# Order of transposes and scores inside an attention step

## The reference

```python
logits = jnp.einsum('bqhd,bkhd->bhqk', q_blk.astype(jnp.float32), kf) * inv_sqrt_d
mask = (key_pos[None, :] < q_pos[:, None])[None, None]
log_beta = jax.nn.log_sigmoid(logits)
log_1m_beta = jnp.where(mask, jax.nn.log_sigmoid(-logits), 0.0)
later = lax.cumsum(log_1m_beta, axis=3, reverse=True) - log_1m_beta
wts = jnp.where(mask, jnp.exp(log_beta + later), 0.0)
return jnp.einsum('bhqk,bkhd->bqhd', wts, vf)
```

## Time and profile before

| | us |
|---|---|
| median of 3 runs | 1737.72 |
| lowest, highest | 1737.65, 1739.27 |
| span of the profiled execution | 1737.0 |
| stage 3 in it, about | 391 to 1367 |
| PE busy in the span | 1674.7 |
| DVE busy in the span | 1156.6 |

### The profile page before, as it was taken

How to read it: one execution, slowest core, us unless ns; L and a number is a source line. 1 busy time by engine, 2 the same in 40 slices (tenths; PEclk the granted TensorE clock), 3 DMA queues, 4 the chain that set the end, 5 groups by cost and what they waited for, 6 DMA issues and landing times. The chain is left out here.

```text
span 1737.0 us, 26738 instructions
## 1 busy us (share of the span) xinstructions
PE 1674.7 (96%) x8430; PEld 1384.2 (80%) x8430; DVE 1156.6 (67%) x1632; ACT 816.9 (47%) x1650; POOL 495.2 (29%) x436
## 2 busy tenths in 40 slices
PE   8999999997999999999989999999999889999998
PEld 6878888886887877888877888878888668888886
DVE  7737400008998899998889988999988674333323
ACT  4412221115676665666656766756766542111111
POOL 3521111104343243242332332432411251505040
PEclk9999999999999999999999999999999999999999
DMA  6621221222221222222213221221213484534331
GB/s 254 224 99 37 74 97 73 72 94 76 71 76 59 62 74 78 69 68 71 79 45 95 78 64 56 86 74 60 73 51 95 146 238 156 146 120 145 121 97 73
DMA packets 103008, 165.99 MB, mean 96 GB/s; under 512 B 27489, under 2 KB 44385, under 8 KB 102881
## 3 DMA queue, kind: packets, MB, share of 16 engines
q1 hardware_dynamic: 102880, 164.45, 30.1%
HBM read 109.89 MB, written 54.53 MB: 95 GB/s over the span
## 5 line engine op out<-in xcount | busy, mean ns | idle before, releaser
L1071 PE MATMUL psum<-hT_hi,w_parts 128*128 128x512 f32 x760 | 315.0, 414 | 0.5 <-POOLq L1397 0.5
L1073 PE MATMUL psum<-hT_lo,w_parts 128*128 128x512 f32 x760 | 310.2, 408 | 0.0
L1075 PE MATMUL psum<-hT_hi,w_parts 128*128 128x512 f32 x760 | 308.3, 406 | 0.0
L1268 DVE TENSOR_TENSOR_SCAN left<-keep,left 128x513 f32<-128x513 f32 x192 | 274.2, 1428 | 30.0 <-ACT keep L1181 28.9
L1181 ACT ACTIVATE keep<-psum 128x512 f32<-128x512 f32 (+3 forms) x320 | 171.3, 535 | 257.4 <-PE psum L1090 155.9
L1275 DVE TENSOR_TENSOR beta<-beta,left 128x512 f32<-128x512 f32 (+3 forms) x320 | 263.6, 824 | 33.4
L1268 DVE TENSOR_TENSOR_SCAN left<-keep 128x513 f32<-128x513 f32 (+3 forms) x128 | 112.3, 877 | 182.7 <-ACT keep L1181 181.7
L1112 PEld LDWEIGHTS psum<-wt,vm 128*128 128x128 f32 x1088 | 165.7, 188 | 74.4 <-DVE wt L1281 41.8
L1112 PE MATMUL psum<-wt,vm 128*128 128x256 f32 x1088 | 187.0, 286 | 28.0 <-DVE wt L1281 27.4
L1191 ACT ACTIVATE wt<-psum 128x512 fp32r<-128x512 f32 (+3 forms) x320 | 171.4, 535 | 59.5 <-PE psum L1101 57.1
L1329 POOL TENSOR_TENSOR y_out<-row_sum 64x128 f32<-64x128 f32 x128 | 62.9, 491 | 466.2 <-DVE row_sum L1290 464.9
(11 more groups left out here) (122 smaller groups left out, 2865.6 us busy)
## 6 DMA issues: line engine op xcount, KB each, us to landing
w_raw<-in_w_strips SPq DMA_DIRECT2D x36, 512.0 KB, 4.2
gate_scratch<-staging SPq DMA_DIRECT2D x64, 256.0 KB, 2.5
gate<-gate_scratch SPq DMA_DIRECT2D x64, 256.0 KB, 4.1
xt<-in_x SPq DMA_DIRECT2D x16, 512.0 KB, 5.1
xT<-in_x_T SPq DMA_DIRECT2D x16, 512.0 KB, 4.0
qk_scratch<-staging SPq DMA_DIRECT2D x32, 256.0 KB, 2.4
k_raw<-qk_scratch SPq DMA_DIRECT2D x64, 128.0 KB, 3.4
q_raw<-qk_scratch SPq DMA_DIRECT2D x128, 64.0 KB, 2.7
```

The source lines that it names most:

```text
L1071: pe.matmul(o, hi, hT_hi[:, kt, tok], start=kt == 0, stop=False)
L1073: pe.matmul(o, hi, hT_lo[:, kt, tok], start=False, stop=False)
L1075: last = pe.matmul(o, lo, hT_hi[:, kt, tok], start=False, stop=kt == KT - 1)
L1268: dve.tensor_tensor_scan(left[:, n % 2, span][:, ::-1], k, k, carry, ALU.mult, ALU.bypass).then_inc(scanned, 1)
```

## The change

In each step of PE's walk the call of `turn` and the call of `score` change places. The order was: score of the newest item, half of the projections, turn of the item two steps older, the rest of the projections, weigh of the item three steps older. It is now: turn, half of the projections, score, the rest, weigh. The instructions, the waits in front of each of them and the other engines' order stay the same.

```diff
                     for n in range(NI):
-                        if pair := here(n):
-                            score(pair, n)
+                        if pair := here(n + T_LAG):
+                            turn(pair, n)
                     while forming and 2 * done < half:
                         next(proj)
                         done += 1
                     for n in range(NI):
-                        if pair := here(n + T_LAG):
-                            turn(pair, n)
+                        if pair := here(n):
+                            score(pair, n)
                     while forming and done < plan[s]:
                         next(proj)
                         done += 1
```

## The result

The changed kernel takes 1838.6 us (median of 4 runs, 1833.5 to 1841.8) against 1738.5 (1737.7 to 1740.2): 1.0567 times as long, 95% interval 1.0549 to 1.0586, 100 us more. The profiled execution has a span of 1836.4 us, 99.4 more than before.

A forecast was written before the change was run, and what follows sets the result against it. PE (96% busy) sets the attention stage's pace, DVE (90%) close behind, in a ring. 1737.7 us plus 84 for the later score, minus 6.5 and 8 of collision relief, gives +69: 1807 us, range 1770 to 1838.

The forecast's parts named there:

- costs that were put at nothing: Everything else, such as matmul pace, operand splits, projection banks, DMAs and the clock granted at 1.00 in the attention stage: 0 us.
- more: Rival, 10%: PE stops before the transposes at the step's head, holding the projections behind them; +100 us, 1838 us.
- The ring and its shift of 1.27 us: Attention stage: PE score, ACT sigmoid, DVE scan, multiply, low part, PE weigh; the score starts 1.27 us later in its step.
- The sum of 84 us: Price of the later score in the attention stage, delays carried through all 320 items: +84 us.
- running delays: Delays of DVE and PE carried item by item against the earlier trace, reduced by backlog and slack; 84 us.
- 66 x 1.27: Second way to the price: 66 places where PE's weight load waits for DVE's low part, times the shift: 84 us.
- The 14.5 us given back: Attention stage: fewer chance collisions of DVE with POOL, 6.5 us, and POOL's mix_t products clear of scans, 8 us.
- The signs to look for: Attention stage: PE idle from 37 to about 105 us, DVE's sigmoid waits from 31.5 to about 100 us.
- the collision part: Relief from DVE and POOL colliding; right if scan's mean falls below 1428 ns and multiply's below 942.
- half of it: Rival, 20% for half or less but still slower: stalls in the attention stage give each other slack; +47 us, 1785 us.
- no change: Rival, 6%: DVE is behind so often in the attention stage that the later sigmoid is covered; 1738 us.
- faster: Rival, 6%: DVE's collisions with POOL clear and PE's 27 us of waits for the low part go; 1711 us.

The follow-up runs named there:

- T H V S R: Changed kernel with the weigh moved on to the next step, directly before the score (turn, half of projections, weigh, score, other half): 1839.3 us.
- H T S R W: Against the kernel before, only the score made late, transposes still in the middle (half of projections, turn, score, other half, weigh): 1836.8 us.
- S H R V T: Against the kernel before, weigh (item n-4) and turn moved to the step's end (score, both halves of projections, weigh, turn): 1706.6 us.
- S V T H R: Against the kernel before, weigh (item n-4) and turn put directly behind the score, then both halves of projections: 1717.9 us.

## Why the prediction was right, and where it was not

The direction, the place and the mechanism held; the size, 69 us, was 31 too small, and 1838.6 lies at the very end of the range, 0.6 above the 1838 that closes it. Of the 31 us, 14.5 are a relief that was counted and did not come, and about 13 are costs that were put at nothing: the slower restart behind a stop and the clock. The remaining 3 us or so are not accounted for. The forecast proper, 1785 to 1830, had been given 58%; the result fell into the part called "more", which had 10%.

- **The ring and its shift of 1.27 us**: right. The two parts run apart put all of it on the late score. The ring's end was named too narrowly, as the weigh alone; the run T H V S R showed that the transposes stand at the same end. In the changed kernel this makes no difference.
- **The sum of 84 us** by the running delays: about right, and right in shape over three sizes (13, 50, 84 against 13, 56, 100). A delay from start to start shows in the trace as idle time and as the uncovered end of the last product before a stop (0.39 us where the next one would have started after 0.23). From the first projection to the last, PE's idle time grew by 70.5 us (34.6 to 105.1) and its stops by 80, whose ends are 80 x 0.16 = 13 us: 83 together. The agreement with 66 x 1.27 was luck, as the prediction said in part: the number of places doubled to 132.
- **The 14.5 us given back**: this term failed, nothing came. The scan's mean is 1424 ns against the 1428 of the earlier trace rows, the multiply's 948 against 942, in these rows of the changed kernel:

```profile
L1268 DVE TENSOR_TENSOR_SCAN left<-keep,left 128x513 f32<-128x513 f32 x192 | 273.4, 1424 | 119.5 <-ACT keep L1181 118.9
L1275 DVE TENSOR_TENSOR beta<-beta,left 128x512 f32<-128x512 f32 x224 | 212.5, 948 | 23.4
```

 The multiply's mean even rose by 6 ns. The collisions are not a matter of chance that thins out with more idle time: 26 scans of 512 keys took over 1.6 us where it had been 28, and of POOL's 16 products with `mix_t` 9 stand beside such a scan, the same 9 in both kernels. POOL's work starts on events of the ring, ACT's splits behind the sigmoids and DVE's own product, so it moves with the scan. The product of step 91 shows it: the prediction left POOL's start where it was and moved the scan alone. In fact DVE's product L1295 stands behind the multiply of item 90, which moved as well. So POOL started at 700.03, 0.29 us before the scan, where it had started 0.09 us before it, and the scan again took long, 2.10 us instead of 2.28.
- **What was left out**: the cost of a stop beyond its wait. Behind a wait four weigh products take 0.58 us instead of 0.48 (median of some 70 places in the changed kernel), one product 0.22 instead of 0.12, two 0.34 instead of 0.24; 80 more stops make 8 us. The clock's falls are 6.7 us instead of 1.4. The new waits before the transposes for the multiply, which the prediction kept for its larger rival, are 1.3 us and stand in the idle time. 83 + 8 + 5.3 = 96, where the stage grew by 97 from its first projection to its last. Both the 8 and the 5.3 are estimates from the distances between starts.
- **The clock**: I wrote that 1.00 is granted in the stage although PE waits. That is a mean over 976 us. A row of before for one microsecond behind the 3.9 us wait, which ended at 879.88, shows the half clock:

```profile
881.00:882.00 1.00, 1.00 (x4) 0.76 (x3) 0.55 (x1) 1.00 (x3) 0.00 (x0) 0.50 0.00 0
```

- **The signs to look for**: PE idle was put at about 105 and is 107, but the part of the loss that shows as busy time (28 us: the ends of the last products before a stop, 13, the slower restart, 8, and the clock, 5) was not foreseen. So the idle time fitted 69 us of loss and the stage grew by 99: this agreement was luck too. DVE's waits for the sigmoid were put at about 100 us in more than 100 places and are 139.5 us in 161. The distance from the second score product to the sigmoid stayed 0.43 us, and the stretches outside stayed at 392 and 369 us. Of the two signs of the collision part, the scan's mean fell by 4 ns and the multiply's did not fall.
- **The rivals**: "half of it", "no change" and "faster" are out. "More" gave the right number, 1838, by 89 us of whole rounds and 10 us of waits before the transposes; the latter measured 1.3 us, and H T S R W, whose transposes are not early, is as slow (1836.8). So its number was right and its mechanism was not.

## What to carry to other kernels

Where two engines feed each other in a ring with double buffers, ask of every reordering on one of them by how much it shortens the way from where the ring leaves that engine to the first instruction that needs anything back, a buffer's release as much as data; the busy shares (96% and 90% here) tell only how little reserve there is. Lengthening that way cost nothing in these runs, where what stands behind the release of a buffer moved back with it: moving the weigh and the transposes that need the same low part together gave 32 us. When a loss is estimated from waits, add for each stop what does not show as idle time, and take relief from collisions off only where the two engines' starts really part.

## What the runs showed of the hardware

- A stop of PE costs more than the wait: the restarted weigh group takes 0.10 us longer, whether it has one, two or four products (four transposes behind a wait in T H V S R only 0.03 us, 0.384 instead of 0.354), and the product before the stop shows its full 0.39 us instead of 0.23. From the first projection to the last, the busy time in the order of before was 930 us with 12 us idle (without POOL's reads) and 938 with 35, in the changed order 954 with 69 (without POOL's reads) and 965 with 105, all with the same matmuls. The clock's falls are part of that.
- The half clock (0.50, 1.2 GHz) came with single waits of 1.8 to 4 us in a stage in which PE is busy by 90%: four times in the changed kernel, once in the kernel before, never within the stage in S H R V T and S V T H R. It did not come with every such wait.
- A product of 512 columns behind one of 128 columns takes 0.28 (behind the mask product) to 0.32 us (behind transposes) to the next start instead of 0.23. Putting short ones together gave 6 us.
- With most of POOL's reads replaced by memsets the collisions all but vanished (the multiply from 942 to 693 ns, the scan from 1428 to 1318): POOL's memsets did not hold DVE.
